# Projecting q, k and v beside the RWKV pairs with 64-row tiles of TensorE

## The reference, cut to what matters

```python
proj = xn @ w_in[l]
dq, dk, dv, rr, rk, rv = jnp.split(proj, split_at, axis=-1)
o_da = diff_attention(dq..., dk..., dv..., lam, da_subln_g[l], lam_init)
o_rw = rwkv7_time_mix(xn, rr, rk, rv, ...)

# inside rwkv7_time_mix, per head, over 256 tokens:
sa = jnp.einsum('bhij,bhj->bhi', state, -kk_t)
state = (state * w_t[:, :, None, :] + sa[..., None] * b_t[:, :, None, :]
         + v_t[..., None] * k_t[:, :, None, :])
y = jnp.einsum('bhij,bhj->bhi', state, r_t)
# then
mean = jnp.mean(y, axis=-1, keepdims=True)
var = jnp.mean(jnp.square(y - mean), axis=-1, keepdims=True)
y = ((y - mean) * lax.rsqrt(var + LN_X_EPS) * ln_w + ln_b)
y = y + jnp.sum(r_h * k_h * r_k, axis=-1, keepdims=True) * v_h   # the bonus
```

## Time and profile before

| | us |
|---|---|
| median of 3 runs | 1630.88 (1629.79 to 1632.81) |
| the profiled execution, its own time | 1631.9 |
| its span in the trace | 1629.8 |
| PE busy (x9348 passes) | 1352.0 (83%) |
| PEld busy | 706.8 (43%) |
| DVE busy | 462.8 (28%) |
| ACT busy | 321.9 (20%) |
| mean granted TensorE clock | 0.932 of full speed |

### The profile page before, as it was taken

The page is one execution under the profiler, slowest core; times in us unless marked ns, Lnnn a source line. Parts: engine busy times, 40 slices in busy tenths (PEclk is TensorE's granted clock), DMA queues, the critical chain, the costliest instruction groups (busy, mean ns, idle before and its releaser), DMA issues.

```text
span 1629.8 us, 22704 instructions
## 1 busy us (share of the span) xinstructions
PE 1352.0 (83%) x9348; PEld 706.8 (43%) x9348; DVE 462.8 (28%) x1080; ACT 321.9 (20%) x741; POOL 39.6 (2%) x88
## 2 busy tenths in 40 slices
PE   7999989999999989897867867866777777777764
PEld 6887878888887444531311312212222222222211
DVE  5031266667752652221101201201102102011003
ACT  2012212333322331121211201111111111110112
POOL 1000001000010000000000000000000000000000
PEclk9999999999999999997988988989889888988987
DMA  9433322222223428679999999999999999999995
GB/s 305 149 104 104 103 78 79 79 79 79 79 79 120 145 80 326 267 327 428 427 429 428 429 429 428 429 428 429 429 428 429 428 429 429 428 429 427 429 427 232
DMA packets 75591, 481.06 MB, mean 295 GB/s; under 512 B 10069, under 2 KB 29158, under 8 KB 50438
## 3 DMA queue, kind: packets, MB, share of 16 engines
q1 hardware_dynamic: 74642, 478.90, 72.8%
q10 hardware_dynamic: 884, 1.23, 0.2%
HBM read 478.01 MB, written 2.10 MB: 295 GB/s over the span
## 4 chain that ended last, share of the span: by engine, by line
PE 50%; DMA 44%; DVE 4%; ACT 1%; issue 1%; DVEq 0%; POOL 0%; SPq 0%
DMA ring<-in_moe_w_up_dram 37%; PE ps L901 11%; PE ps L722 9%; PE ps L980 6%; PE ps L1128 5%; DMA ring<-in_moe_w_gate_dram 4%; PE ps L1103 3%; PE ps L1147 2%; DMA ring<-in_moe_w_down_dram 2%; PE ps L792 2%; PE ps L1155 1%; PE ps L930 1%; PE ps L1139 1%; PE ps L742 1%; PE ps L780 1%
## 5 line engine op out<-in xcount | busy, mean ns | idle before, releaser
L1128 PE MATMUL ps<-ring,oT 128*32 128x512 f32 x2048 | 318.6, 756 | 224.1 <-DMA ring<-in_moe_w_gate_dram 112.9
L1128 PEld LDWEIGHTS ps<-ring,oT 128*32 128x32 f32 x2048 | 64.8, 123 | 462.2 <-issue 185.0
L901 PE MATMUL ps<-xT,ring 128*128 128x256 f32 x768 | 190.7, 391 | 0.0
L1997 DVE TENSOR_TENSOR oT<-oT,ps 128x128 f32<-128x128 f32 x32 | 9.2, 288 | 628.7 <-ACT oT L1491 628.7
L901 PEld LDWEIGHTS ps<-xT,ring 128*128 128x128 f32 x768 | 138.6, 189 | 23.5 <-issue 3.6
L722 PE MATMUL ps<-xT,ring 128*128 128x256 f32 x640 | 139.2, 380 | 0.3 <-DVE xT L1558 0.3
L722 PEld LDWEIGHTS ps<-xT,ring 128*128 128x128 f32 x640 | 121.3, 190 | 18.0 <-issue 1.6
L1147 PE MATMUL ps<-ring,oT 128*32 128x512 f32 x1024 | 118.1, 601 | 8.6 <-DVE oT L1997 8.1
L1103 PE MATMUL ps<-xT,oT 128*32 128x512 f32 x512 | 123.6, 1095 | 0.0
L980 PE MATMUL ps<-ring,oT 128*128 128x512 f32 x256 | 114.2, 597 | 1.9 <-DVE oT L1774 1.1
L1483 ACT COPY oT<-ps 128x512 f32<-128x512 f32 x32 | 18.7, 585 | 406.1 <-PE ps L1128 406.1
(11 more groups left out here) (316 smaller groups left out, 1229.9 us busy)
## 6 DMA issues: line engine op xcount, KB each, us to landing
ring<-in_moe_w_gate_dram SPq DMA_DIRECT2D x64, 2048.0 KB, 33.7
ring<-in_moe_w_up_dram SPq DMA_DIRECT2D x64, 2048.0 KB, 35.8
ring<-in_moe_w_down_dram SPq DMA_DIRECT2D x64, 2048.0 KB, 35.9
ring<-in_w_in_dram SPq DMA_DIRECT2D x24, 1024.0 KB, 5.2
ring<-in_w_in_dram SPq DMA_DIRECT2D x32, 768.0 KB, 4.7
ring<-in_w_out_dram SPq DMA_DIRECT2D x16, 1024.0 KB, 5.2
res<-in_x_dram SPq DMA_DIRECT2D x2, 1024.0 KB, 6.6
out_dram<-oT SPq DMA_DIRECT2D x4, 512.0 KB, 3.0
```

The source lines that it names most:

```text
L901: last = mm(ps[:, 6 + (par + c) % 2, 0:S], wv[:, k, c * P:(c + 1) * P], xT[:, kq * KQ + k, :], start=(kq == 0 and k == 0), stop=(kq == 3 a ...
L1128: last = mm(ps[c * B:(c + 1) * B, 1 + j % 2, :], xe[:, par, 8 * (j // 2) + k, :], w[:, k, :], start=(j < 2 and kq == 0), stop=(j >= 2 and ...
```

## The change

`project` splits each matmul of 128 rows into two of 64 rows, rows 0 to 63 into bank 6 and rows 64 to 127 into bank 7. Both halves of a block fill both banks, and their sum is the block. ACT copies bank 6 into `projA` as it did; DVE copies bank 7 into a new buffer `qhalf` (`qkv_half`) and adds it to `projA` once ACT's copy is there (`qkv_sum`). So a new block may start only when both banks of the block just finished are read. `bonus`, `group_mean` and `group_variance` of the loop become two 64x64 tiles each, the latter two in the unused halves of banks 1 and 3, between the solve step and the inverse step.

```diff
             def bonus(q, par):
                 pe.wait_ge(r_am, q * 4 + 4)
-                mm(ps[:, 0, 0:S], same64[:, :], rkrs[par], start=True, stop=True).then_inc(r_bo, 1)
+                for rows in heads:
+                    last = mm(ps[rows, 0, 0:S], same64[rows, rows], rkrs[par][rows, :], start=True, stop=True)
+                last.then_inc(r_bo, 1)
...
                     if kq == 0 and half == 0:
-                        pe.wait_ge(s_paA, p * 3 + c + 2)
-                        if p == 0 and c == 1:
+                        pe.wait_ge(s_paA, p * 3 + c + 3)
+                        pe.wait_ge(s_paB, p * 3 + c)
+                        if p == 0 and c == 0:
                             pe.wait_ge(s_prA, 4 * RB + 4)
-                        if p > 1 and c == 0:
-                            pe.wait_ge(s_vo, p - 1)
-                        if p > 0 and c == 2:
-                            pe.wait_ge(s_cen, p)
...
                     for k in (2 * half, 2 * half + 1):
-                        last = mm(ps[:, 6 + (par + c) % 2, 0:S], wv[:, k, c * P:(c + 1) * P], xT[:, kq * KQ + k, :],
-                                  start=(kq == 0 and k == 0), stop=(kq == 3 and k == KQ - 1))
+                        for h, rows in enumerate(heads):
+                            last = mm(ps[:, 6 + h, 0:S], wv[rows, k, c * P:(c + 1) * P], xT[rows, kq * KQ + k, :],
+                                      start=(kq == 0 and k == 0), stop=(kq == 3 and k == KQ - 1))
...
+            def group_mean_tiles(m):
+                for rows in heads:
+                    last = mm(ps[rows, 1, S:2 * S], same64[rows, rows], oT[rows, MT + m, :], start=True, stop=True)
+                last.then_inc(s_mean, 1)
...
                 for k in range(12):
+                    if p and k == 8:
+                        pe.wait_ge(s_cen, p)
+                    if p and k == 11:
+                        pe.wait_ge(s_vo, p)
                     solve(p, par, k)
+                    if p and k == 5:
+                        group_mean_tiles(p - 1)
+                    if p and k == 9:
+                        group_variance_tiles(p - 1)
...
                     project(p, par, k)
-                    if p and k == 5:
-                        pe.wait_ge(s_paA, p * 3 + 4)
-                        group_mean(p - 1, 6 + par, S)
-                    if p and k == 9:
-                        pe.wait_ge(s_paA, p * 3 + 5)
-                        group_variance(p - 1, 7 - par, S)
...
             group_mean(MT - 1, 2, 0)
-            pe.wait_ge(s_paA, 3 * MT + 3)
+            pe.wait_ge(s_paC, 3 * MT)
...
+            def qkv_half(p, c):
+                if c < 2:
+                    dve.wait_ge(s_pa, p * 2 + c + 1)
+                else:
+                    dve.wait_ge(s_free, p * 4 + (4 * RB + 4))
+                dve.wait_ge(s_paC, p * 3 + c)
+                v.tensor_copy(qhalf, ps[:, 7, 0:S]).then_inc(s_paB, 1)
+
+            def qkv_sum(p, c):
+                dve.wait_ge(s_paA, p * 3 + c + 4)
+                dve.wait_ge(s_paB, p * 3 + c + 1)
+                at = projA[:, p * 3 + c, :]
+                v.tensor_tensor(at, at, qhalf, ALU.add).then_inc(s_paC, 1)
...
                 for k in range(12):
+                    if k in (4, 8):
+                        qkv_half(p, k // 4 - 1)
                     if k < 11:
                         solve_copy(p, par, k)
+                    if k in (4, 8):
+                        qkv_sum(p, k // 4 - 1)
+                    if k == 0 and p:
+                        qkv_sum(p - 1, 2)
...
                 else:
                     mix_last(2 * p + 1)
+                qkv_half(p, 2)
```

More of the change, by code:

```diff
@@ L110, in hybrid_layer @@
         ones = sb("ones", [P, P])
+        qhalf = sb("qhalf", [P, S])[:, :]
         vec = sb("vec", [P, 161])
@@ L295, in hybrid_layer @@
         s_pa = sem("qkv_block_projected")
+        s_paB = sem("qkv_half_copied")
+        s_paC = sem("qkv_halves_added")
         s_paA = sem("qkv_block_copied")
@@ L944, in group_variance, with group_variance_tiles @@
                 mm(ps[:, bank, at:at + S], same64[:, :], projR[:, m, :], start=True, stop=True).then_inc(s_var, 1)
+            def group_mean_tiles(m):
+                for rows in heads:
+                    last = mm(ps[rows, 1, S:2 * S], same64[rows, rows], oT[rows, MT + m, :], start=True, stop=True)
+                last.then_inc(s_mean, 1)
+            def group_variance_tiles(m):
+                pe.wait_ge(s_csq, m + 1)
+                for rows in heads:
+                    last = mm(ps[rows, 3, S:2 * S], same64[rows, rows], projR[rows, m, :], start=True, stop=True)
+                last.then_inc(s_var, 1)
             def pair(p, par, more=True):
@@ L1364, in qkv_copy @@
                     act.wait_ge(s_free, p * 4 + (4 * RB + 4))
-                a.copy(projA[:, one(p * 3 + c), :], ps[:, 6 + (par + c) % 2, 0:S]).then_inc(s_paA, 1)
+                a.copy(projA[:, one(p * 3 + c), :], ps[:, 6, 0:S]).then_inc(s_paA, 1)
             def group_squares(m):
@@ L1811, in pair @@
                     if p and k == 6:
-                        centre(p - 1, 6 + par, S)
+                        centre(p - 1, 1, S)
                     if p and k == 10:
-                        variance(p - 1, 7 - par, S)
+                        variance(p - 1, 3, S)
                     if k == 9:
@@ L1829, in pair @@
                     mix_last(2 * p + 1)
+                qkv_half(p, 2)
             for p in range(MT):
                 pair(p, p % 2, more=(p < MT - 1), prep=(p < MT - 2))
+            qkv_sum(MT - 1, 2)
             dve.wait_ge(s_dist, DIST_STEPS)
```

## The result

The changed kernel takes 1639.73 us (median of 5, 1639.06 to 1640.46), the kernel before on the same chip 1629.79 us (median of 5, 1629.55 to 1632.81). The ratio is 1.0054 with a 95% interval of 1.0040 to 1.0068: about 9 us slower, clear of noise though small. The profiled execution's span is 1638.6 us, 8.8 more than before. Part of the distance to the forecast of 1642 us is its base: the forecast was built on a kernel before of 1630.9 us, and the one that ran beside the changed kernel took 1629.8.

A forecast was written before the change was run, and what follows sets the result against it. The pairs were taken as bound by PE, the last stage by the weights' transfers. Terms 0 + 1.2 + 6.5 + 0.4 + 1.6 + 0.7 + 0.5 = 10.9 us on 1630.9 gave 1642 us; range 1617 to 1650, this case's own 1638 to 1649.

The forecast's parts named there:

- The form of the tiles: Projection on PE: 64x64 to 64x128 still costs a full change of form, so gain 0, bounds 0 and 33 us.
- the faster rival: Forms with 64 rows mix freely on PE: 33 us go, 8 come back in waits, 1617 us; chance 0.18.
- The passes: Projection on PE: 16 passes a step take what eight took, except 0 to 2.3 us; 1.2 us taken.
- the drift: Projection steps: second tile's later start and a few ns a pass, 0 to 0.024 us a step, 1.2 us taken.
- The small sums: Bonus and 14 group sums as 64x64 tiles keep their 0.22 a pass and change no count of rounds: 0.
- The waits: PE waits at block starts for copies: 6.5 us at step 4, 0.4 at step 8, 1.6 in pair 8.
- DVE's margin at step 5: DVE's `power` ends 0.3 us before PE needs it for step 5's inverse, so it costs 0.
- The pair's end: DVE's added copy and add delay mask products and bonus, 0.33 us late in two pairs; 0.7 us in all.
- The end of the stage: Attention's first scores wait for DVE's last add instead of ACT's copy: 0.5 us.
- free mixing: Same case as the faster rival: changes among tiles of 64 rows cost nothing, 1617 us; chance 0.18.

The follow-up runs named there:

- e4: The changed kernel with each 64x128 projection tile split by columns into two of 64x64, leaving no change of form inside the pairs: 1616.4 us, ratio 0.9908.
- e7: e4 with the bonus and norm sums back as one 128x128 matmul each, at the changed kernel's places: 1621.5 us, ratio 0.9949 to the kernel before.
- e2: The kernel before with only the loop's bonus and norm sums as 64x64 tiles at their new places, projection untouched: 1632.1 us, ratio 1.0001.
- e3: The kernel before with one wait number changed, so a block's first matmul waits for ACT's copy of the block just before it: 1639.9 us, ratio 1.0050.
- e1: The changed kernel with ACT's copy of bank 6 moved ahead of its power copy at step 4: 1633.3 us, ratio 1.0017 to the kernel before.

## Why the prediction was right

**The form of the tiles.** The term was 0 of a possible 33 us, drawn from a change of columns alone. The trace after shows it, 0.07 ahead instead of 0.16, and e4 and e7 show that the price was there to be saved: the case that I gave as the faster rival, 1617 us, is what e4 measured at 1616.4, by taking the changes of form away instead of hoping that they are free among tiles of 64 rows. That the numbers are so close is partly luck: the 33 us were right, but that sum also held 1.2 + 0.7 us for two terms that turned out near zero, below, and gave back 8 us where the steps of e4 lost 9 to 10. The drain that the Trainium skill names ("TensorEngine Tiling (Array Packing)", section Key Properties) is borne out here for 64x64 and 64x128 too.

**The passes.** I took 1.2 us for the drift, and it isn't there: the 71 steps without a wait are 0.25 us longer in all, though each group of passes is shown as 2.00 us instead of 1.99. The side-by-side run holds in a stream of 16 passes and in one of 32. The small sums, which I had put at 0, cost 0.6 us at the bonus (e2), so the two errors offset each other in part.

**The waits.** 6.5 + 0.4 + 1.6 = 8.5 us were forecast; e3, which has these waits alone, lengthens the stage by 8.6, and in the changed kernel the three terms read 6.6, 0.4 and 1.7. At step 4 PE starts 0.05 us after ACT's copy, as I took it from the bonus of pair 1. DVE's margin at step 5 was not 0.3 us but 371.48 - 370.43 = 1.05: I had left out that the group mean's tiles now run ahead of this inverse, which moves it 0.43 us back, and had added DVE's durations where its instructions overlap, which is the next point.

**The pair's end.** This term was mis-sized. I had the bonus late by 0.33 us in two pairs, 0.7 in all; in the trace these two pairs lose 0.02 us each against the others. DVE's rows there are:

```profile
391.97 0.42 DVE L1790 TENSOR_TENSOR oT<-oT,ring 128x256 f32<-128x256 f32 x1
392.32 0.41 DVE L1809 COPY qhalf<-ps 128x256 f32<-128x256 f32 x1
392.65 0.21 DVE L1797 COPY ring<-ps 64x64 f32<-64x64 f32 x1
392.83 0.42 DVE L1815 TENSOR_TENSOR ring<-ring,qhalf 128x256 f32<-128x256 f32 x1
393.18 2.84 DVE L1689 TENSOR_TENSOR wk<-ps,mask 64x512 f32<-64x512 f32 x4
```

From the last group output to the mask products it is 1.21 us for four instructions whose durations sum to 1.46. Independent instructions on DVE start some 0.35 us apart while each is shown as 0.42; I had added durations, and gaps on top. The rows for this were in front of me: the solve copy at 390.08 begins before the 390.17 at which the group output ends. My chain had the mask products 1.57 us behind the start of the last group output (389.74 to 391.31), and they came 1.21 behind it.

**The end of the stage.** 0.5 us forecast; PE waited 0.4 for the last add. It is not part of the 9.7 us, since it comes behind the projection's last pass.

The sum was 10.9 and the medians differ by 9.9. The large term, ACT's copy at step 4, and the two other waits are shown by e3; the 1 us between the sums is 1.2 + 0.7 us too much for drift and pair's end, and 0.6 too little for the bonus, with a few tenths elsewhere. The chance of 0.18 for free mixing was too high for what the rows said: they held each dimension's change at full price, and I left room only because the exact pair of forms was missing.

## What to carry to other kernels

Read the price of a change of tile form from start to start in the trace, and then ask whether an edit takes changes away or only makes the two forms more alike: here, alike in rows saved nothing, equal in both dimensions saved 23 us. A price per round is fully paid back only in steps where nothing else is late; here 33 us of changes gave 24, and the rest went into waits. A wait that is added for a second reader of a buffer costs what stands ahead of that reader in its engine's order, so look there first; e1 won back two thirds of the loss by exchanging two copies on ACT. On an engine whose instructions overlap, chains are added up from start to start, never from durations.

## What the runs showed of the hardware that was not expected

Four 64x64 tiles with 256 moving columns each run side by side in float32 for 32 passes without a loss (1.96 us; a stream of 8 passes at 128x128 takes 1.99), and without a change of form their first passes start among the last passes of the group before (362.48 to 362.49 in e4). A round from 64x64 tiles to another form and back costs about 0.35 us: 0.34 by the rows of before (128x128), 0.34 to 0.35 in the 64 undisturbed steps by which e4 and the changed kernel differ (64x128), and 0.36 at each of e7's 14 group sums (128x128). Where PE waits for another engine at that place, less of it is seen, 0.19 at e7's bonuses.
